# Latent attention: the value product as three rounded passes over two query tiles, in place of one full-precision product per tile

## The reference, cut to what matters

```
def head_group_inputs(h, w_in, g_q, w_uq, g_kv, w_ukv):
    ...
    q = (rms_norm(c_q, g_q) @ w_uq).reshape(B, L, MLA_HEADS, MLA_NOPE + MLA_ROPE)
    kv = (rms_norm(c_kv, g_kv) @ w_ukv).reshape(B, L, MLA_HEADS, MLA_NOPE + MLA_V)
    ...
    k_nope, m_v = kv[..., :MLA_NOPE], kv[..., MLA_NOPE:]

def attend(q, k, v):
    s = jnp.einsum('bqhd,bkhd->bhqk', q, k).astype(jnp.float32) * (1.0 / math.sqrt(q.shape[-1]))
    p = jax.nn.softmax(s, axis=-1)
    return jnp.einsum('bhqk,bkhe->bqhe', p.astype(v.dtype), v)

def blocked_attention(q, k, v):
    ...
    out = lax.map(lambda qi: attend(qi, k, v), qb)
    return out.swapaxes(0, 1).reshape(B, L, H, v.shape[-1])

        y_mla = blocked_attention(q_m, jnp.concatenate([k_mc, k_m], axis=1),
                                  jnp.concatenate([mvc, mv], axis=1)).reshape(B, L, MLA_HEADS * MLA_V)
```

## Time and profile before

| what | before |
|---|---|
| median of 3 runs | 2749.9 us (2749.69 to 2751.81) |
| the profiled execution | 2746.85 us |
| its span, first to last instruction | 2745.0 us |
| mean granted TensorE clock in it | 0.988 of full speed |
| PE busy in the whole span | 2630.6 us (96%) |
| DVE, ACT, POOL busy | 1460.4, 1060.6, 480.2 us |
| loop of the latent attention | about 496 to 699 us of the span |
| value product (L2143) records, PE | 640 |

### The profile page before, as it was taken

How to read it: one execution, slowest core, us unless ns; L and a number is a source line. 1 busy time by engine, 2 the same in 40 slices (tenths; PEclk the granted TensorE clock), 3 DMA queues, 4 the chain that set the end, 5 groups by cost and what they waited for, 6 DMA issues and landing times. The chain is left out here.

```text
span 2745.0 us, 36345 instructions
## 1 busy us (share of the span) xinstructions
PE 2630.6 (96%) x14641; PEld 2282.5 (83%) x14641; DVE 1460.4 (53%) x2041; ACT 1060.6 (39%) x1788; POOL 480.2 (17%) x321
## 2 busy tenths in 40 slices
PE   6999979999999999999999999999999999999999
PEld 2777767899777888888888999878989998878977
DVE  5745483333457666666657624447743624426751
ACT  3411534443335343343345224247731223237740
POOL 0001211242100000000000001038820002009930
PEclk9999989999999999999999999999999999999999
DMA  5542101000211121121121315232122213233222
GB/s 238 174 140 101 55 5 54 16 1 1 100 47 42 51 62 47 47 62 47 46 62 41 109 43 124 59 93 56 44 95 92 66 49 86 59 108 83 48 85 84
DMA packets 69683, 193.68 MB, mean 71 GB/s; under 512 B 8080, under 2 KB 26896, under 8 KB 68624
## 3 DMA queue, kind: packets, MB, share of 16 engines
q1 hardware_dynamic: 69520, 191.41, 23.0%
HBM read 148.88 MB, written 19.07 MB: 61 GB/s over the span
## 5 line engine op out<-in xcount | busy, mean ns | idle before, releaser
L2677 DVE SCALAR_TENSOR_TENSOR res<-ps,gates,res 128x1024 f32<-128x1024 f32 x120 | 148.6, 1279 | 100.0 <-PE ps L2802 100.0
L1315 PE MATMUL ps<-h_hi,pf_wh 128*128 128x346 f32 (+2 forms) x800 | 184.5, 334 | 0.2
L2536 ACT ACTIVATE wo_wh<-ff_raw 128x512 fp32r<-128x512 f32 x120 | 75.3, 628 | 278.7 <-DVE ff_raw L2647 114.2
L1315 PE MATMUL ps<-h_lo,pf_wh 128*128 128x346 f32 (+2 forms) x800 | 183.0, 333 | 0.0
L1946 DVE TENSOR_REDUCE da_negmax<-ps 128x1 f32<-128x1040 f32 x136 | 167.5, 1236 | 18.8 <-PE ps L1796 11.6
L1931 POOL TENSOR_TENSOR da_E<-da_E,da_F 128x1040 f32<-128x1040 f32 x68 | 164.6, 2421 | 5.7
L2802 PE MATMUL ps<-ff_h_hi,wo_wh 128*128 128x512 f32 x512 | 157.8, 389 | 1.4 <-DVE res L2677 1.3
L1839 PE MATMUL ps<-da_aT,v 128*128 128x128 f32 (+1 forms) x1224 | 157.5, 274 | 0.7 <-ACT qk L1903 0.7
L2802 PE MATMUL ps<-ff_h_hi,wo_wl 128*128 128x512 f32 x512 | 157.6, 389 | 0.0
L2802 PE MATMUL ps<-ff_h_lo,wo_wh 128*128 128x512 f32 x512 | 157.6, 389 | 0.0
L905 POOL MEMSET h_hi<- 128x112 f32 x2 | 0.4, 194 | 870.8 <-POOLq L66 870.8
(11 more groups left out here) (546 smaller groups left out, 6227.2 us busy)
## 6 DMA issues: line engine op xcount, KB each, us to landing
ff_raw<-w_ff SPq DMA_DIRECT2D x48, 512.0 KB, 3.5
ada_w<-w_ada SPq DMA_DIRECT2D x16, 1024.0 KB, 7.4
ff_raw<-w_in SPq DMA_DIRECT2D x20, 512.0 KB, 4.1
pf_raw<-w_in SPq DMA_DIRECT2D x20, 512.0 KB, 4.0
wo_raw<-w_out SPq DMA_DIRECT2D x18, 512.0 KB, 4.6
residual_spill<-res SPq DMA_DIRECT2D x16, 520.0 KB, 3.1
st_q<-st_q_rounded SPq DMA_DIRECT2D x32, 260.0 KB, 5.2
ada_w<-w_ada SPq DMA_DIRECT2D x4, 2048.0 KB, 17.0
```

Of the source, the lines that this page charges most:

```text
L1315: pe.matmul(bank(i * 2 + s, s)[c], wh[:, s, q * P:(q + 1) * P], x(q)[:, a:a + ln], start=(q == 0 and n == 0), stop=False)
L2536: act.activation(ring(wh, i), src, ACT.Copy).then_inc(s_hi, 1)
L2677: last = dve.scalar_tensor_tensor(out=res[:, m, :], in0=k.ps[:, b:b + 2, :].rearrange("p c w -> p (c w)"), scalar=gate[:, m:m + 1], in1=re ...
```

## The change

- `gemm_tokens("mv")` now gets two output tiles, `mla_v_hi` and `mla_v_lo`, so ACT writes the rounded part of the values and DVE the rest.
- The turned weights are kept for a pair of query tiles, as `mla_aT_hi` and `mla_aT_lo`, each 10 by 2 by 128 wide and there once (the two float32 tiles of before alternated). ACT copies all three batches to the rounded tile; DVE subtracts all three batches to the rest tile, each behind ACT's copy.
- `pv` runs only behind the second tile of a pair. It makes 30 passes of 256 columns, three for each of ten key tiles.
- ACT copies the result of a pair at once, 256 columns.
- ACT's copy of batch 1 stands ahead of the exponential in its list. DVE's subtraction of batch 2 stands ahead of the maximum.
- The waits follow: a bank of turned weights is free when DVE's subtraction is done (`s_lo`), the value product waits for the subtractions of its second tile, and batch 0 of the first tile of a pair waits on ACT for the last value product.

```diff
@@ L2084 @@
     bank = (6, 7, 6)
     with phase(nc):
         E = [k.sb(f"{name}_E{i}", [P, n_keys], e0 + i * (4 * n_keys + 32)) for i in range(3)]
-        aT = [k.sb(f"{name}_aT{i}", [P, NT, P], at0 + i * NT * 512) for i in range(2)]
+        aT_hi, aT_lo = (k.sb(f"{name}_aT_{n}", [P, NT, 2, P], at0 + i * NT * 1024, F32R) for i, n in enumerate(("hi", "lo")))
         mx = k.sb(f"{name}_max", [P, 4], k.small0)
         nm = k.sb(f"{name}_negmax", [P, 4], k.small0 + 32)
         sums = k.sb(f"{name}_sums", [P, 2], k.small0 + 64)
         rec = k.sb(f"{name}_rec", [P, 2], k.small0 + 128)
         s_S, s_mx, s_nm, s_exp, s_rec, s_A = (k.sem(f"{name}_{n}") for n in ("scores", "max", "negmax", "exp", "rec", "A"))
-        s_T, s_at, s_at1, s_pv, s_o = (k.sem(f"{name}_{n}") for n in ("turned", "aT", "aT_middle", "pv", "o"))
+        s_T, s_hi, s_lo, s_pv, s_o = (k.sem(f"{name}_{n}") for n in ("turned", "aT_hi", "aT_lo", "pv", "o"))
         splits.open(s_S, NQ, 0)
         with nc.Block() as block:
             @block.sync
@@ L2121 @@
                         pe.wait_ge(s_A, g + 1)
                         if g:
 
-                            pe.wait_ge(s_at, 2 * g)
+                            pe.wait_ge(s_lo, 3 * g)
                     elif b == 1:
-                        if g:
-
-                            pe.wait_ge(s_o, g)
+                        if g >= 2 and g % 2 == 0:
+
+                            pe.wait_ge(s_o, g // 2)
                     else:
 
-                        pe.wait_ge(s_at, 2 * g + 1)
+                        pe.wait_ge(s_lo, 3 * g + 1)
                     for j, t in enumerate(batch[b]):
                         tr = pe.transpose(k.ps[:, bank[b], j * P:(j + 1) * P], E[g % 3][:, t * P:(t + 1) * P], k.ident[:])
                     tr.then_inc(s_T, 1)
 
                 def pv(g):
 
-                    pe.wait_ge(s_at1, g + 1)
-                    pe.wait_ge(s_at, 2 * g + 1)
+                    h = g // NQ
+                    pe.wait_ge(s_lo, 3 * g + 2)
                     for t in range(NT):
                         if t == 8:
-                            pe.wait_ge(s_at, 2 * g + 2)
-                        mm = pe.matmul(k.ps[:, 7, 0:P], v(g // NQ, t), aT[g % 2][:, t, :], start=(t == 0), stop=(t == NT - 1))
+                            pe.wait_ge(s_lo, 3 * g + 3)
+                        for n, (x, a) in enumerate(((v(0, h, t), aT_hi), (v(0, h, t), aT_lo), (v(1, h, t), aT_hi))):
+                            mm = pe.matmul(k.ps[:, 7, 0:2 * P], x, a[:, t].rearrange("p g q -> p (g q)"),
+                                           start=(t == 0 and n == 0), stop=(t == NT - 1 and n == 2))
                     mm.then_inc(s_pv, 1)
 
                 busy(pe, k, 7, 22)
@@ L2155 @@
                         scores(g, False)
                     if i >= 0:
                         turn(i, 2)
-                        pv(i)
-
-            def evacuate(eng, g, b, sem):
-                eng.wait_ge(s_T, 3 * g + b + 1)
-                if b < 2 and g >= 2:
-
-                    eng.wait_ge(s_pv, g - 1)
+                        if i % 2:
+                            pv(i)
+
+            def turned(g, b):
                 nb = len(batch[b])
-                dst = aT[g % 2][:, 4 * b:4 * b + nb, :]
-                src = k.ps[:, bank[b], 0:nb * P].rearrange("p (t q) -> p t q", t=nb)
-                (eng.activation(dst, src, ACT.Copy) if sem is s_at else eng.tensor_copy(dst, src)).then_inc(sem, 1)
+                hi, lo = (x[:, 4 * b:4 * b + nb, g % 2, :] for x in (aT_hi, aT_lo))
+                return hi, lo, k.ps[:, bank[b], 0:nb * P].rearrange("p (t q) -> p t q", t=nb)
 
             @block.scalar
             def _(act):
@@ L2180 @@
                     act.activation(E[g % 3][:], window(g), ACT.Exp, bias=nm[:, g % 4:g % 4 + 1], scale=scale,
                                    accum_out=sums[:, g % 2:g % 2 + 1]).then_inc(s_exp, 1)
 
+                def round_turned(g, b):
+                    hi, _, src = turned(g, b)
+                    act.wait_ge(s_T, 3 * g + b + 1)
+                    if g >= 2 and b == 0:
+
+                        act.wait_ge(s_pv, g // 2)
+                    act.activation(hi, src, ACT.Copy).then_inc(s_hi, 1)
+
                 def out(g):
-                    act.wait_ge(s_pv, g + 1)
-                    act.activation(o_dst(g // NQ, (g % NQ) * P, P), k.ps[:, 7, 0:P], ACT.Copy).then_inc(s_o, 1)
+                    act.wait_ge(s_pv, g // 2 + 1)
+                    act.activation(o_dst(g // NQ, (g % NQ - 1) * P, 2 * P), k.ps[:, 7, 0:2 * P], ACT.Copy).then_inc(s_o, 1)
 
                 for x in range(splits.ACT_STEPS):
                     splits.round(act, 0, x)
                 for g in range(NG + LAG + 1):
                     i = g - LAG
-                    if i >= 1:
+                    if i >= 2 and i % 2 == 0:
                         out(i - 1)
                     if 0 <= i < NG:
-                        evacuate(act, i, 0, s_at)
+                        round_turned(i, 0)
+                        round_turned(i, 1)
                     if 1 <= g <= NG:
                         exps(g - 1)
                     if 0 <= i < NG:
-                        evacuate(act, i, 2, s_at)
+                        round_turned(i, 2)
                     if g < NG and g // NQ + 1 < heads and 1 <= g % NQ <= splits.ACT_STEPS:
                         splits.round(act, g // NQ + 1, g % NQ - 1)
 
@@ L2210 @@
 
             @block.vector
             def _(dve):
+                def rest_turned(g, b):
+                    hi, lo, src = turned(g, b)
+                    dve.wait_ge(s_hi, 3 * g + b + 1)
+                    dve.tensor_tensor(lo, src, hi.bitcast(F32), ALU.subtract).then_inc(s_lo, 1)
+
                 for x in range(splits.REST_STEPS):
                     splits.rest(dve, 0, x)
                 for g in range(NG + LAG):
                     i = g - LAG
                     if i >= 0:
-                        evacuate(dve, i, 1, s_at1)
+                        rest_turned(i, 0)
+                        rest_turned(i, 1)
                     if 1 <= g <= NG:
 
                         dve.wait_ge(s_exp, g)
@@ L2224 @@
                             dve.wait_ge(s_A, g - 2)
                         r = slice((g - 1) % 2, (g - 1) % 2 + 1)
                         dve.reciprocal(rec[:, r], sums[:, r]).then_inc(s_rec, 1)
+                    if i >= 0:
+                        rest_turned(i, 2)
                     if g < NG:
                         if g >= 4:
 
@@ L2307 @@
     qh, ql, kh, kl = normed
     rows = lambda w: (lambda m: w[bass.ds(m * P, P), :])
     v0 = F0 + 6 * L * 4
-    v = k.sb("mla_v", [P, LT // P, MH * MV], v0)
+    vh, vl = (k.sb(f"mla_v_{n}", [P, LT // P, MH * MV], v0 + i * (LT // P) * MH * MV * 4, F32R) for i, n in enumerate(("hi", "lo")))
     h0 = v0 + 2 * (LT // P) * MH * MV * 4
     k_at = [h0 + i * 5152 for i in range(4)]
     kraw = k.sb("k_nope", [P, MH, LT], h0 + 4 * 5152)
@@ L2316 @@
          evac_act=copy_out(lambda m, a, w: kraw[:, m, a:a + w] if isinstance(m, int) else kraw[:, bass.ds(m, 1), a:a + w], call))
     gemm_tokens(nc, k, "mv", lambda q: d["w_mv"][q * P:(q + 1) * P, :], 2, MH * MV,
                 lambda q, a: kh[:, q, a:a + P], lambda q, a: kl[:, q, a:a + P],
-                list(range(0, LT, P)), lambda t: (v[:, t, :],), preloaded=True, behind=4, then=("uq", rows(d["w_uq"]), 3 * P, 2))
+                list(range(0, LT, P)), lambda t: (vh[:, t, :], vl[:, t, :]), preloaded=True, behind=4, then=("uq", rows(d["w_uq"]), 3 * P, 2))
     qpe = k.sb("q_pe", [P, MH, L], k.res0 - 512)
 
     def out_queries(act, m, s, i, banks, freed, first):
@@ L2330 @@
 
     q_at = [k.ring0 + 3 * 5152 + i * 4 * L for i in range(2)] + [F0 + i * 4 * L for i in range(6)]
     splits = LatentSplits(k, lambda h: y[:, h, :], lambda h: qpe[:, h, :], lambda h: kraw[:, h, :], keys.ks, q_at, k_at)
-    latent_heads(nc, k, "mla", MH, L // P, splits, LT, lambda h, t: v[:, t, h * MV:(h + 1) * MV], 1.0 / math.sqrt(NOPE + ROPE),
+    latent_heads(nc, k, "mla", MH, L // P, splits, LT, lambda r, h, t: (vh, vl)[r][:, t, h * MV:(h + 1) * MV], 1.0 / math.sqrt(NOPE + ROPE),
                  lambda h, a, w: y[:, h, a:a + w], k.ring0, at0, ("wo1", rows(d["w_out"]), KD * P, 2), k.res0 + 25088)
 
 
```

## The result

| | before | changed |
|---|---|---|
| median | 2749.8 us (8 runs, 2743.56 to 2753.01) | 2760.42 us (8 runs, 2756.92 to 2767.13) |
| ratio, 95% interval | | 1.0039, 1.0030 to 1.0048 |
| the profiled execution, its span | 2746.85, 2745.0 us | 2761.66, 2759.8 us |

The forecast was 2760.2 us. The new value product is cheaper on TensorE, and the kernel is slower by 0.39%.

A forecast was written before the change was run, and what follows sets the result against it. PE, busy 201.3 of 202.8 us in the loop, was taken as the bound. Fifteen pairs +7.4, last pair +2.7 and "mv" +0.2 make +10.3 us: 2757.2 for the profiled execution, 2760.2 as median, range 2753 to 2768.

The forecast's parts named there:

- Passes: Value product on PE: 30 passes of 256 columns at 0.1186 us, 3.56 a pair; PE's own work falls by 0.92.
- Rival A: Passes at 0.109 us and restarts without weight-load loss: either alone leaves +5.3 or +5.7 us, both +0.7; chance 0.12.
- First wait: In every step without a value product, PE's early scores wait 0.85 us for ACT's exponential, behind two copies.
- Rival B: The exponential does not hold PE up, so the kernel is faster: -10.9 us, 2739.0 us; chance 0.04.
- Second and third wait: PE waits for DVE's subtractions: batch 2's transposes 0.09 us every step, the value product 0.38 every second step.
- Per pair: Two loop steps: PE's work plus waits is 12.95 us against 12.46 before, 0.49 longer; fifteen pairs give +7.4.
- t0: Start of ACT's first copy in a loop step, from which the prediction counts times in us.
- Covered items: In the loop, batch 2's subtraction (cover 1.8 and 1.0 us), the maximum and POOL's scaling finish before PE needs them.
- "mv": Ten subtractions added on DVE, each 0.69 us behind a copy; only 0.2 us comes through.
- The last pair: Loop's end, no scores as cover: last tile's transposes wait for POOL, 2.7 us later than PE could; +2.7 us.
- C: DVE's new subtractions and POOL block each other, so PE waits longer: 2774 to 2779 us; chance 0.06.
- D: A 256-column pass is issued as two records like float32: 50 us more, 2811 us; chance 0.02.

The follow-up runs named there:

- e7: Changed kernel with the value product's third pass (low part of the values) left out, so two passes per key tile; 0.9966 of the kernel before.
- e1: Changed kernel with ACT's exponential and DVE's reciprocal moved first in the steps without a value product; 0.9978 of the kernel before.
- e5: Changed kernel with pairs of tiles kept but weights and values in plain float32, no subtractions; 1.0046 of the kernel before.
- e2: Changed kernel with a tile's ten transposes in batches of 3, 4 and 3 in place of 4, 4 and 2; 1.0015 of the kernel before.
- e4: Changed kernel with ACT's exponential between the copies of batches 0 and 1, as in the kernel before; 1.0126 of the kernel before.
- e9: Changed kernel with 11 spare products ahead of the last tile's transposes; not timed, end 17.34 us in the trace against 19.24 in the changed kernel.
- e10: e3 with spare products (3, 1, 5 and 3) in PE's idle times of the last two steps; 0.9972 of the kernel before.
- e3: Changed kernel with exponential first in steps without a value product and batches of 3, 4 and 3; 2739.65 us, 0.9974 of the kernel before.
- e6: Changed kernel with three rounded passes for one tile of 128 columns at a time, in every step; 1.0184 of the kernel before.

## Why the prediction was right, point by point

- **Passes.** Forecast 0.1186 each; starts are 0.1190 apart, and e7 gives 0.119 by taking ten away. The Trainium skill (TensorE: Matmul & The Clock Gate, Back-to-back issue gap) gives 0.109 for 256 columns, for matmuls alone, without the weight load that each pass here has; the measurement is a tenth above it and decides. Rival A falls: the passes are not cheaper, and nor are restarts, since the nine scores that waited (573.37) last 2.01 and the nine that did not (568.54) 1.91.
- **First wait, the exponential.** Forecast 0.85; measured 0.87, fifteen times, and e1 takes 0.89 a pair away by removing it. The mechanism is shown: with the value product absent there is no cover, also in float32 (e5). Rival B falls.
- **Second and third wait, the subtractions.** Forecast 0.09 a step and 0.38 a pair, so 0.47 in the long step; measured 0.46 there. e2 shows that they are waits for subtractions that stand in a queue, though of its 0.43 a pair about 0.15 are the exponential coming sooner.
- **Per pair** 12.95 forecast, 12.96 measured. (The prediction read the early scores at t0+3.85; its row has 570.90, t0+3.76, so the cover before was 1.86, not 1.95. No term of the sum used it.) From the first score to the transposes of the last tile but one the loop is 7.4 us longer, which is the term of the sum.
- **Covered items.** The subtraction of batch 2, the maximum and POOL's scaling never ended a wait of PE inside the loop, as said. e4 shows what happens when that cover goes: the value product and the scaling both hold PE up.
- **"mv".** Forecast +0.2, measured +0.2: it starts 1.1 us later than before, ahead of which nothing was changed, and the product behind it 1.3 later.
- **The last pair** was mis-sized: forecast +2.7, measured +4.6 (19.24 against 14.60). The step that failed is the stretch behind the wait for POOL, reckoned at the loop's full pace: transposes at 5.06, value product "7.78 to 11.34". The wait was there as forecast and the transposes started at 4.91, but the clock had fallen, and the value product ran from 8.29 to 13.30, its first dozen passes 0.213 apart in place of 0.119. Of the 1.9 us, 0.7 lie in the last tile's transposes and 1.2 in its value product. e9 shows it: with the clock kept it is 4.91, and 7.58 to 11.41, and the end is +2.74.
- **Contention and two records (C, D).** Subtractions of 0.687 and 0.425 in the mean and 0.694 at most, with POOL at work beside them, and 480 records: neither came about. The 0.05 per copy and subtraction that the range allowed for stepped writes came from no row; at 596 and 687 ns the new ones took nothing of it.
- **The whole.** In the traces the loop takes 12.0 more and "mv" 0.2, so 12.2 against a sum of 10.3; the last pair's 1.9 makes the difference. The medians are 10.6 apart, the two profiled executions 14.8, and single executions of either kernel scatter by 9 to 10. What lies behind the loop, untouched by the change, takes 2040.9 us in the trace of before, 2042.3 after and between 2039.0 and 2046.5 in those of the experiments, so the match of the whole to 0.2 us is luck, while the match of the pair is not.

## What to carry to other kernels

Before an operation is thinned out, made rarer or batched, ask what it was covering: here the value product hid the exponential. Halving how often it runs cost 0.87 us a pair, nearly all of the 0.9 that the cheaper passes gave (30 of 0.119 for 40 records of 0.112), and the waits for the added subtractions made it a loss. When the cover comes in every second step, the other engines' lists should differ between odd and even steps too. Where a tail without cover lets PE idle, its granted clock belongs in the sum; here a few spare products, counted to fit the idle times, kept it (e9, e10). What they are worth in timed runs was too small to tell.

## What the runs showed of the hardware

- The clock fell without a long wait. In e3 PE idled for at most 1.26 us at a time at the loop's end, and the clock was at its lower level from about 684.4 to 687.8, as the windows below give it (e10's expectation names the shorter stretch of its slow passes, 2.9 us from 684.7); e10 filled these idle times and it stayed. The Trainium skill (TensorE: Matmul & The Clock Gate, A second HAM failure mode: psum-queue depth-cycling) tells of another kernel in which short, frequent idle times between groups of matmuls let the clock swing. e3 and e10 agree in that short idle times were enough; here the clock fell once.
- A rounded pass costs nearly the same for 128 and 256 columns (0.113 us in e6, 0.119 in the changed kernel), a float32 record nearly double (0.112 before, 0.216 in e5).

The windows of e3 (the clock is the number behind POOL's):

```profile
684.00:686.00 2.00, 1.87 (x10) 1.63 (x10) 1.03 (x2) 0.49 (x1) 0.00 (x0) 0.60 0.00 0
686.00:688.00 2.00, 2.00 (x12) 2.00 (x12) 0.00 (x0) 0.00 (x0) 0.00 (x0) 0.54 0.00 0
```
